# The first two output pairs of each down-projection chunk, computed in step

## The reference, cut to what matters

```
f = rmsnorm(h, norm_ffn)
h = h + (jax.nn.silu(f @ w_gate) * (f @ w_up)) @ w_down
```

## Time and profile before

| | |
|---|---|
| median of 3 runs | 2971.16 us (2970.48 to 2980.84) |
| profiled execution, its own time | 2986.34 us |
| its span | 2984.5 us |
| TensorE matmul busy | 2789.6 us, 93% |
| TensorE weight load busy | 2653.1 us, 89% |
| VectorE busy | 1705.2 us, 57% |
| ScalarE busy | 1024.3 us, 34% |
| mean granted TensorE clock | 0.964 |
| HBM traffic | 319.11 MB read, 68.00 MB written |

### The profile page before, as it was taken

The page is one execution under the profiler, slowest core; times in us unless marked ns, Lnnn a source line. Parts: engine busy times, 40 slices in busy tenths (PEclk is TensorE's granted clock), DMA queues, the critical chain, the costliest instruction groups (busy, mean ns, idle before and its releaser), DMA issues.

```text
span 2984.5 us, 49258 instructions
## 1 busy us (share of the span) xinstructions
PE 2789.6 (93%) x20329; PEld 2653.1 (89%) x20329; DVE 1705.2 (57%) x2517; ACT 1024.3 (34%) x1518; POOL 392.6 (13%) x166
## 2 busy tenths in 40 slices
PE   7999999999999987997799999999999999999997
PEld 7987898877777765997799999999999989999997
DVE  3321599444444445114777777777766687777423
ACT  5223221323333323223434334334334353443322
POOL 2222233211111101332000000000000000000231
PEclk9999999999999997998899999999999999999999
DMA  6322231555555545442243343343333364654521
GB/s 217 110 68 78 69 108 48 161 156 145 160 157 148 151 122 182 133 133 81 67 135 117 115 132 117 117 130 117 118 120 101 105 232 149 214 173 153 208 101 64
DMA packets 394447, 388.80 MB, mean 130 GB/s; under 512 B 25405, under 2 KB 354725, under 8 KB 391160
## 3 DMA queue, kind: packets, MB, share of 16 engines
q1 hardware_dynamic: 367112, 360.00, 38.4%
q10 hardware_dynamic: 27120, 25.77, 2.5%
HBM read 319.11 MB, written 68.00 MB: 130 GB/s over the span
## 4 chain that ended last, share of the span: by engine, by line
PE 55%; DVE 4%; issue 1%; ACT 1%; DMA 0%; ACTq 0%; POOL 0%; SPq 0%; DVEq 0%
PE PS L1335 43%; PE PS L890 7%; PE PS L1317 5%; DVE xo_t L2462 0%; DMA xr_x<-opS 0%; DVE XR L2423 0%; DVE WL L2314 0%; ACT xo_x L1802 0%; DVE xo_t L2428 0%; DVE xo_x L2428 0%; DVE y_out L2509 0%; DVE xo_x L2462 0%; DVE mx L2289 0%; DVE W L2314 0%; DVE AL L2162 0%
## 5 line engine op out<-in xcount | busy, mean ns | idle before, releaser
L1335 PE MATMUL PS<-xo_t,WH 128*128 128x288 f32 x2560 | 522.4, 298 | 21.2 <-ACT kept L1739 10.0
L890 PE MATMUL PS<-AH,WH 128*128 128x288 f32 (+1 forms) x2208 | 496.6, 307 | 23.0 <-POOL WL L803 5.4
L890 PE MATMUL PS<-AL,WH 128*128 128x288 f32 (+1 forms) x2208 | 483.8, 301 | 0.0
L890 PE MATMUL PS<-AH,WL 128*128 128x288 f32 (+1 forms) x2208 | 482.2, 301 | 0.0
L1335 PEld LDWEIGHTS PS<-xo_t,WH 128*128 128x128 f32 x2560 | 417.3, 191 | 22.8 <-issue 22.8
L890 PEld LDWEIGHTS PS<-AH,WH 128*128 128x128 f32 (+1 forms) x2208 | 367.2, 195 | 46.0 <-issue 28.0
L1335 PE MATMUL PS<-xo_x,WH 128*128 128x288 f32 x1920 | 387.7, 296 | 13.4 <-DVE xo_x L2428 13.2
L1335 PE MATMUL PS<-xo_t,WL 128*128 128x288 f32 x1280 | 380.9, 298 | 0.0
L890 PEld LDWEIGHTS PS<-AL,WH 128*128 128x128 f32 (+1 forms) x2208 | 367.1, 195 | 0.0
L890 PEld LDWEIGHTS PS<-AH,WL 128*128 128x128 f32 (+1 forms) x2208 | 365.4, 194 | 0.0
L2314 DVE TENSOR_TENSOR WL<-WRAW,WH 128x1024 fp32r<-128x1024 f32 x200 | 244.7, 1224 | 139.4 <-ACT WH L1731 138.1
(11 more groups left out here) (370 smaller groups left out, 3632.5 us busy)
## 6 DMA issues: line engine op xcount, KB each, us to landing
WRAW<-in_w_gate SPq DMA_DIRECT2D x22, 2048.0 KB
WRAW<-in_w_up SPq DMA_DIRECT2D x22, 2048.0 KB
WRAW<-in_w_down SPq DMA_DIRECT2D x32, 1024.0 KB
WRAW<-in_w_in SPq DMA_DIRECT2D x14, 2048.0 KB, 8.3
raw<-in_w_in SPq DMA_DIRECT2D x48, 512.0 KB, 4.1
kca<-in_cache_k SPq DMA_DIRECT2D x256, 64.0 KB, 2.8
vca<-in_cache_v SPq DMA_DIRECT2D x256, 64.0 KB, 2.0
WRAW<-in_w_out SPq DMA_DIRECT2D x16, 1024.0 KB, 10.5
```

The source lines that it names most:

```text
L890: last = nc.tensor.matmul(G[gslot][0:width, h, 0:HALF], wt[:, half if slot is None else slot, k % 8, 0:width], act[:, k, h * HALF:(h + 1) ...
L1335: last = mm(out, wt[:, k, :], act[:, m, k, :], start=(j in (0, 1, 3) and k == 0 and wt is wh and m == 0), stop=(k == 7 and wt is wl), skip ...
```

## The change

For the first two pairs of each chunk (44 and 45, 52 and 53) the fourteen products are put in another order, `COUPLE`: (0,0) (1,0) (0,1) (1,1) (0,2) (1,2) (0,3) (1,3) (0,4) (0,5) (0,6) (1,4) (1,5) (1,6), where the first number is the pair within the two. In what follows these are places 0 to 13. The turns of the operands now come in every second window: operand j in window 7q - 4 + 2j. Three `keep`s of the second pair are moved to later windows, because `kept` has one place for each kind. On SyncE the weights of the second pair are loaded after the fifth operand, and the sixth and seventh operand after the loads and stores of the sums.

```diff
--- before.py
+++ after.py
@@ -373,10 +373,20 @@
         FIRST = (NPAIR, NPAIR + 8)
+        COUPLE = ((0, 0), (1, 0), (0, 1), (1, 1), (0, 2), (1, 2), (0, 3), (1, 3), (0, 4), (0, 5), (0, 6), (1, 4), (1, 5), (1, 6))
         seq = [(q, j) for q in range(NALL) for j in range(7)]
+        for q in FIRST:
+            seq[7 * q:7 * q + 14] = [(q + d, j) for d, j in COUPLE]
+        keeps = {c + 1: [v] for c, v in enumerate(seq) if v[1] in (0, 2, 3)}
+        for q in FIRST:
+            for was, now, v in ((2, 4, (q + 1, 0)), (8, 10, (q + 1, 3)), (6, 10, (q + 1, 2))):
+                keeps[7 * q + was].remove(v)
+                keeps.setdefault(7 * q + now, []).append(v)
         POS = {v: c for c, v in enumerate(seq)}
         ADD = {v: n + 1 for n, v in enumerate(v for v in seq if v[1] in (1, 4, 5, 6))}
-        KEEP = {v: n + 1 for n, v in enumerate(v for v in seq if v[1] in (0, 2, 3))}
+        for c, now in keeps.items():
+            now.sort(key=lambda v: v != seq[c - 1])
+        KEEP = {v: n + 1 for n, v in enumerate(v for c in range(1, 7 * NALL + 1) for v in keeps.get(c, ()))}
@@ -717,18 +727,19 @@
-                for j in range(7):
+                for j in range(5):
                     load_operand(e, j)
+                load_weights(q + 1)
                 if e == 0:
                     store_hidden(NPAIR // 2 - 1)
                     load_sums(q)
-                    load_weights(q + 1)
                     sp.wait_ge(s["h_st"], 16 * (NPAIR // 2))
                     load_sums(q + 1)
                 else:
-                    load_weights(q + 1)
                     store_sums(q - 1)
                     next_sums(q - 1)
+                for j in range(5, 7):
+                    load_operand(e, j)
@@ -1746,12 +1757,16 @@
             def window(c):
 
-                q1, j1 = seq[c - 1]
-                if j1 in (0, 2, 3):
-                    keep(q1, j1, q1 % 2)
+                now = keeps.get(c, ())
+                late = [v for v in now if v != seq[c - 1]]
+                for q1, j1 in now:
+                    if (q1, j1) not in late:
+                        keep(q1, j1, q1 % 2)
                 if c + 2 < NPROD:
                     q2, j2 = seq[c + 2]
                     cast(c + 2, q2, j2, (c + 2) % 3, q2 % 2)
+                for q1, j1 in late:
+                    keep(q1, j1, q1 % 2)
@@ -1796,8 +1811,8 @@
             def turn_high(e, n):
 
-                j = n + 4
-                if 0 <= j < 7:
+                j = (n + 4) // 2
+                if n % 2 == 0 and 0 <= j < 7:
```

## The result

The changed kernel takes 2984.53 us (median of 20 runs, 2977.92 to 3000.55) against 2971.68 for the kernel before (20 runs, 2968.09 to 2989.52): ratio 1.0043, 95% interval 1.0031 to 1.0055, which is 12.8 us slower. The forecast was 2983.4, +12.2.

The account below looks back on a forecast made before the run. TensorE sets the pace and loses 23.5 us at the two chunk starts. Afterwards 16.0 + 17.3 + 1.4, plus 1 for hand-overs, makes 35.7: +12.2 us, 2983.4 on the median, range 2974 to 2993.

Parts of the forecast that it names:

- Part (1): Chunk starts: turns spread over 13 windows give VectorE 46.1 us for TensorE's 41.6, about 4.5 us of overload a chunk.
- the rival built on it: Both chunk starts: weights arrive in time, only some 5 us of overload a chunk stays; -13 us, 2958, chance 0.07.
- (3): Places 1 to 5: VectorE's ledger of 22.4 and 21.2 us makes place 5 late by 14.2 and 15.5 us.
- Part (2): Place 1: second pair's weights, queued behind five operands, come 10.1 and 12.5 us after ScalarE wants them.
- fast-weights rival: Second pair's weights: load queued behind operands flows at their rate; +6 in place of +12, 2977, chance 0.12.
- The tail behind place 5: Behind place 5 in each chunk: low clock loses 1.5 us, small waits 0.3.
- The landing: Second pair's weights ready for ScalarE, semaphore included, at 2421.0 in the first chunk and 2613.7 in the second.
- the 1.4 and the 1 us: Added: 1.4 us for the second chunk's (51, 6) stall and third pair's weights, 1 us for missed small hand-overs.
- the +9: Upper bound on the forecast's error from weight data, semaphore time and low clock; -8 to +9 us was taken.
- the clock rival: Chunk starts: low clock isn't all hidden or lasts longer, third pair's weights late; +15 to +22, 2990, chance 0.28.
- Weights in time: Data through by 2411 and 2601, so only some 5 us of overload a chunk stays; -13 us, 2958, chance 0.07.
- Nothing moves: Chunk starts: VectorE's savings pay for late weights, stall at place 1, none at 5; within 5 us, 2971, chance 0.10.

Follow-up runs that it names:

- e2: Changed kernel, but only one eighth of the rows of the second pair's weights loaded in each chunk: 2974.67 us, ratio 1.0003 to the kernel before.
- cheap-turn runs: Changed kernel with one eighth of each new operand loaded and turned: 2969.07 us; the same with one eighth of the second pair's weights too: 2949.08 us.
- e1: Changed kernel with the second pair's weights issued behind the third operand instead of the fifth: 2981.42 us, ratio 1.0028 to the kernel before.
- e3: Changed kernel with only one eighth of each new operand loaded and turned, weights loaded in full: 2969.07 us, ratio 0.9982 to the kernel before.
- e9: The changed kernel itself, unedited, run again beside other runs on the same chip: 2985.64 us, ratio 1.0041 to the kernel before.

## Why the prediction was right, and where its sum was off

**What is lost, and where.** Right: the chunk starts alone changed. 23.5 us became 39.4.

**Part (1), spread turns.** Its 4.5 us of overload a chunk was far too mild as a bound for what is left when the weights are in time: the rival built on it stood at -13 us, and e2, which is nearly that case, came out at 0, with some 3 us still to be won by its trace. The average over 13 windows hides where the load stands. In e2 VectorE is through with the work before place 1 at 2407.3, and place 5 was due at 2423.4 (nine products behind the end of the long run, 2394.6): 16.1 us, into which 22.9 us of its ledger have to go, from `low_w` of place 1 to the start of place 5. The prediction's own ledger in (3) had this; its rival did not use it. In the cheap-turn runs the 5.1 and 4.5 us in front of place 5 fell to 1.5.

**Part (2), late weights.** Right that they are late, nearly right in size, and wrong in how much of it is the queue. SyncE issued them at 2406.06 where ScalarE asked at 2408.35, and ScalarE waited 11.5 and 12.7 us, forecast 10.1 and 12.5. Shifted by the 2.6 us by which this execution came earlier, the first landed 1.5 us later than forecast. No row stood behind the 0.8 us from the last byte to the semaphore; here bytes still moved at 2419.5 and the cast began at 2419.89. The rate was 269 GB/s behind full-speed operands, so queueing the load didn't speed it up and the fast-weights rival falls; the rule of the Trainium skill behind it ("DMA: Bandwidth & Descriptors", Specifications: line rate from pieces of 512 B on) is not what these pieces of 1 KB did, though no run shows whether it is their size that slows them. The issue was held by the free slot (2404.82 + 1.23 for `low_w`, then SyncE at 2406.06), and not by the fifth operand, as I had it; the two times nearly coincide, and e1 tells them apart: with two operands fewer ahead the issue came no earlier, and 9.1 and 10.9 us of the wait stayed. The forecast gave the queue 4 us in the first chunk (issue at 2408.2, operands through at 2412.2) and closed with "anything that lets those 2 MB overtake the operands takes both stalls away". That step failed: with two operands overtaken (e1) the stalls were 6.6 and 7.7, 5.4 and 4.5 us, and with seven eighths of the operand bytes gone (e3) ScalarE still waited 9.4 and 10.5 us, and place 1 5.3 and 6.3. The queue is worth about 2 us a chunk; the late slot and a load of some 10 us are the rest, and place 5's stall comes from VectorE.

**Part (3), VectorE's ledger.** From `low_w` of place 1 to the start of place 5 it is 22.9 us in the first chunk (2420.97 to 2443.89), forecast 22.4, and 23.1 in the second (2620.55 to 2643.63), forecast 21.2. Place 5 was late by 16.2 and 18.2 us, forecast 14.2 and 15.5. **Two terms were too small here, by about as much each.** Of the 2.0 us more in the first chunk 1.5 are the later landing of part (2) and 0.5 the ledger; of the 2.7 us more in the second 0.8 and 1.9. 1.5 us of the ledger's excess in the second is the wait of `second` for place 1 at 1.2 GHz. The prediction held that the low clock at places 1 to 4 is hidden by VectorE's backlog; it is only where no VectorE instruction in that backlog waits for TensorE.

**The tail behind place 5.** 2.65 us and 2.3 us, forecast 1.8 each, clock and small waits: 1.3 more in both.

**The sum.** 39.4 us lost, forecast 35.7. The landing was 2.3 us short, the ledger 2.4 and the tail 1.3, together some 6; the 1.4 and the 1 us that the forecast added for the small rest weren't needed and took 2.4 of it back. The part of the time that two traces compare grew by 15.3 us (13.9 in e9), the measured medians by 12.8, the forecast said 12.2. So that forecast and median are 1 us apart is luck in part: by the traces it was short by 2 to 4 us, inside the +9 allowed for them, and the clock rival had the sign of the error and overstated it.

**The other rivals.** "Weights in time" was named for the other side; by e2 and its trace it would reach some 3 us under before and not 13. "Nothing moves" asked for no stall at place 5, and that stall was there in every run with full turns in this order. The gain that was expected of the second chunk's (51, 6), 3.43 to 0.9 us, came.

## What to carry to other kernels

Reordering work so that one operand serves two consumers brings the second consumer's other input forward as well; write down for each what is now needed first, when its buffer comes free, how long its load takes by itself and what stands ahead of it in the DMA queue, before counting what the spreading wins. Here the free slot and the load's own length made most of the lateness, and the queue about 2 us. The changed order took the second pair's first use from place 7 to 1 and lost 13 us; with it at place 3 the kernel won 8 to 12. An average load over a stretch does not price it; a ledger from the late event to the next thing that TensorE waits for does, and it must contain the waits of the busy engine for TensorE too, since the granted clock was at 0.50 behind the stall of 9.5 us and the slow product then held VectorE for 1.55 us. A named releaser is a place to look, no price: moving the keep ahead won nothing.

## Not expected

The two causes added up almost to the microsecond (15.3 and 20.9 us apart, 36.5 together), though both work through one engine's order. And the low clock behind the stalls went away when the waits were filled with 56 and 36 matmuls that nobody reads: the granted clock was 1.00 in place of 0.81 and 0.83, and product (45, 0) took 3.2 us in place of 4.4. That changed the traces by 3.5 to 4.7 us and no measured time for certain.
